# A hybrid decoder step on one core: cache pages one chunk sooner, two weight chunks back to back, Exps and merged values in other places

## What is computed

```python
xn = rms_norm(x, norm_w)
aq, ak, av, az, mq, mk, mv, mo, mz, ga, gm, mi, mf = split(xn @ w_in)
aq, ak = partial_rope(rms_norm(aq)), partial_rope(rms_norm(ak))
attn = moba(aq, ak, av)                     # samples: q . cached keys, top 3 of 4 blocks, softmax, cached values
h, (C, n, m) = mlstm_chunk(...)             # C_new = a * C + k v, h = q C / max(|q n|, exp(-m))
h = rms_norm(h * sigmoid(mo))
y_att = (attn * silu(az)) @ w_proj_attn
y_ml  = (h * silu(mz)) @ w_proj_mlstm
y = x + (sigmoid(ga) * y_att + sigmoid(gm) * y_ml) @ w_out
```

## Time and profile before

| | |
|---|---|
| median of three runs | 494.61 us |
| the profiled execution's own time | 493.16 us |
| its span in the trace | 491.4 us |
| TensorE matmul, busy | 464.9 us, 95% |
| VectorE busy | 403.6 us, 82% |
| ScalarE busy | 290.2 us, 59% |
| GpSimd busy | 102.2 us, 21% |
| the chain that ended last | TensorE 66%, VectorE 21%, ScalarE 5%, issue 4%, DMA 3% |

### The profile page before, as it was taken

The page is one execution under the profiler, slowest core; times in us unless marked ns, Lnnn a source line. Parts: engine busy times, 40 slices in busy tenths (PEclk is TensorE's granted clock), DMA queues, the critical chain, the costliest instruction groups (busy, mean ns, idle before and its releaser), DMA issues.

```text
span 491.4 us, 11313 instructions
## 1 busy us (share of the span) xinstructions
PE 464.9 (95%) x3848; PEld 422.5 (86%) x3848; DVE 403.6 (82%) x1650; ACT 290.2 (59%) x486; POOL 102.2 (21%) x182
## 2 busy tenths in 40 slices
PE   3899997999989999998999999999999999989997
PEld 2699897899869899887899889799989898889997
DVE  2988859799999889979889889889999864657861
ACT  2776544577884466795456595666678367324430
POOL 2032121102323213332421323222223210000000
PEclk9999999899999999999999999999999999999999
DMA  8498567847899998999988999997999995354511
GB/s 310 168 378 301 209 246 258 305 173 241 305 419 412 394 343 286 356 418 391 413 333 300 365 410 397 414 383 273 349 420 414 412 415 228 147 222 173 192 63 45
DMA packets 36409, 150.87 MB, mean 307 GB/s; under 512 B 5232, under 2 KB 6772, under 8 KB 29056
## 3 DMA queue, kind: packets, MB, share of 16 engines
q1 hardware_dynamic: 12160, 70.77, 37.6%
q0 software_dynamic: 19040, 67.20, 36.0%
q10 hardware_dynamic: 5152, 12.18, 6.4%
HBM read 137.37 MB, written 12.76 MB: 306 GB/s over the span
## 4 chain that ended last, share of the span: by engine, by line
PE 66%; DVE 21%; ACT 5%; issue 4%; DMA 3%; POOL 0%; ACTq 0%; POOLq 0%; DVEq 0%
PE pj L506 24%; PE pj L509 12%; PE wk L506 8%; DVE kpages L1127 7%; DVE w L1020 5%; PE pa L699 4%; PE wk L509 4%; PE wk L611 2%; PE wk L482 2%; DMA qbc<-q_dram 2%; PE wk L643 1%; DVE cslot L1213 1%; ACT L796 1%; ACT w L775 1%; DMA mlg<-in_tokens 1%
## 5 line engine op out<-in xcount | busy, mean ns | idle before, releaser
L506 PE MATMUL pj<-xn,w 128*128 128x264 f32 x1344 | 187.3, 292 | 3.6 <-issue 2.0
L506 PEld LDWEIGHTS pj<-xn,w 128*128 128x128 f32 x1344 | 171.9, 190 | 16.0 <-issue 11.7
L1020 DVE TENSOR_TENSOR w<-wraw,w 128x1024 fp32r<-128x1024 f32 x112 | 138.0, 1233 | 13.2 <-ACT w L775 12.7
L775 ACT ACTIVATE w<-wraw 128x1024 fp32r<-128x1024 f32 x112 | 117.7, 1052 | 24.0 <-PE wk L509 12.8
L1127 DVE CUSTOM_DVE_ANT_0 kpages<-kpages,qbc 128x128 f32<-128x128 f32 x512 | 115.6, 290 | 6.6 <-POOL qbc L415 4.7
L509 PE MATMUL pj<-xn,w 128*128 128x264 f32 x672 | 94.8, 284 | 0.0
L509 PEld LDWEIGHTS pj<-xn,w 128*128 128x128 f32 x672 | 86.5, 188 | 0.0
L399 POOL DMA_DIRECT2D kpages<-in_cache_k x64 | 34.3, 536 | 190.5 <-DVE sco L1127 157.9
L399 POOL DMA_DIRECT2D vpages<-in_cache_v x64 | 34.0, 531 | 60.7 <-issue 40.5
L1127 DVE DVE_READ_ACCUMULATOR2_ANT sco<- 128x1 f32 x512 | 41.7, 81 | 0.0
L699 PE MATMUL pa<-vpages,prob 128*32 128x256 f32 x512 | 34.3, 385 | 0.4 <-ACT prob L834 0.3
(11 more groups left out here) (262 smaller groups left out, 626.7 us busy)
## 6 DMA issues: line engine op xcount, KB each, us to landing
wraw<-in_weights SPq DMA_DIRECT2D x56, 1024.0 KB, 7.9
kpages<-in_cache_k POOLq DMA_DIRECT2D x64, 512.0 KB, 8.5
vpages<-in_cache_v POOLq DMA_DIRECT2D x64, 512.0 KB, 10.3
cslot<-in_states SPq DMA_DIRECT2D x16, 512.0 KB, 11.0
out_C_s<-cslot ACTq DMA_DIRECT2D x16, 512.0 KB, 9.9
xres<-in_tokens SPq DMA_DIRECT2D x1, 1056.0 KB, 7.6
out_k_p<-kT ACTq DMA_DIRECT2D x4, 256.0 KB, 11.0
out_v_p<-v_nat ACTq DMA_DIRECT2D x4, 256.0 KB, 4.4
```

The source lines that it names most:

```text
L506: mm(bank[:, 0:T], w2[:, q, 0, k, :], src[:, g, k, :], start=(k == 0 and g == 0), stop=False)
L775: A(w2[:, n % WSPLIT, 0], wraw[:, pair % WRAW, :, (n % 2) * P:(n % 2 + 1) * P], ACT.Copy).then_inc(whi_ready, 1)
L1020: V.tensor_tensor(w2[:, q, 1], wraw[:, slot, :, half * P:(half + 1) * P], w2[:, q, 0], ALU.subtract).then_inc(wlo_ready, 1)
```

## The change

Seven edits:

- START goes from 3 to 2 and all lags up by one: the key pages move one chunk sooner, everything behind them stays at its g.
- GpSimd spreads the first query straight from `qs` in SBUF, before it waits for the DRAM copy; the second query is spread inside the loop, at g = 4.
- In the body TensorE keeps the old order for g = 0 and 1. From g = 2 on it does P(g) and P(g + 1) for even g, then S(g) and S(g + 1) (`beside`).
- P(96), the first chunk of the output projection, goes slice by slice: for each k two products of the high weight and one of the low.
- ScalarE's three Exps at i = 1 come after the copy out of the chunk and the next `split_hi`.
- `merged_values` comes ahead of the gate product of g = 87.
- The wait counts of `q_row` follow from the second edit.

```diff
@@ -81,8 +81,8 @@
 
 
 
-START, PERIOD = 3, 9
-SUMS, SELECT, SHIFT, EXP, VALUES, TOTAL, GATHER, COLUMNS, OUT = 8, 9, 10, 11, 12, 14, 19, 20, 21
+START, PERIOD = 2, 9
+SUMS, SELECT, SHIFT, EXP, VALUES, TOTAL, GATHER, COLUMNS, OUT = 9, 10, 11, 12, 13, 15, 20, 21, 22
 
 
 def due(g, lag):
@@ -411,7 +411,7 @@
                 pool.dma_start(qbc[0:1, b % 2, :], q_dram[b:b + 1, :]).then_inc(q_row[b % 2], 16)
 
             def spread_queries(b):
-                pool.wait_ge(q_row[b % 2], 16 * (b // 2 + 1))
+                pool.wait_ge(q_row[b % 2], 16 * ((b + 1) // 2))
                 nc.gpsimd.partition_broadcast(qbc[:, b % 2, :], qbc[0:1, b % 2, :]).then_inc(q_spread, 1)
 
             def decay_rows(j):
@@ -442,13 +442,13 @@
             spread_rows(0)
             pool.wait_ge(qs_ready, 2)
             pool.dma_start(q_dram, qs[:, :]).then_inc(q_put, 16)
+
+            nc.gpsimd.partition_broadcast(qbc[:, 0, :], qs[0:1, :]).then_inc(q_spread, 1)
             pool.wait_ge(q_put, 16)
-
+            queries(1)
+
+            pool.wait_ge(q_spread, 1)
             values(VSLOTS - 1)
-            queries(0)
-            queries(1)
-            spread_queries(0)
-            spread_queries(1)
 
             for g in range(LAST):
                 b = due(g, SELECT)
@@ -461,7 +461,7 @@
                         keys(s + KSLOTS)
                     if s % PAGES == 0 and 2 <= s // PAGES + 1 < NB:
                         queries(s // PAGES + 1)
-                    if s % PAGES == 2 and 2 <= s // PAGES + 1 < NB:
+                    if s % PAGES == 2 and s // PAGES + 1 < NB:
                         spread_queries(s // PAGES + 1)
                 pair = value_pair(g)
                 if pair is not None:
@@ -498,6 +498,15 @@
 
                 pe.wait_ge(whi_ready, n + 1)
                 q = n % WSPLIT
+                if src is mrg2 and parts:
+                    pe.wait_ge(wlo_ready, n + 1)
+                    for k in range(KC):
+                        pe.wait_ge(parts, k + 1)
+                        mm(bank[:, 0:T], w2[:, q, 0, k, :], src[:, 0, k, :], start=(k == 0), stop=False)
+                        mm(bank[:, 0:T], w2[:, q, 1, k, :], src[:, 0, k, :], start=False, stop=False)
+                        last = mm(bank[:, 0:T], w2[:, q, 0, k, :], src[:, 1, k, :], start=False, stop=(k == KC - 1))
+                    last.then_inc(proj, 1)
+                    return
                 for k in range(KC):
                     if parts:
 
@@ -700,9 +709,8 @@
                                       vpages[:, s % VSLOTS, q * VW:(q + 1) * VW], start=(pg == 0), stop=(pg == PAGES - 1))
                         last.then_inc(v_used, 1)
 
-            for g in range(BODY):
-                pe.wait_ge(evac, HEADS + g - 1)
-                project(pj[g % 2], HEADS + g, xn2)
+            def beside(g):
+
                 if g == 0:
                     pe.wait_ge(q_ready, HEADS)
                     query_rows(pa[1], 0)
@@ -720,6 +728,15 @@
                 keys_side(g // CHUNKS, g % CHUNKS)
                 states_side(g // CHUNKS, g % CHUNKS)
                 cache_side(g)
+
+            for g in range(BODY):
+                pe.wait_ge(evac, HEADS + g - 1)
+                project(pj[g % 2], HEADS + g, xn2)
+                if g < 2:
+                    beside(g)
+                elif g % 2:
+                    beside(g - 1)
+                    beside(g)
 
 
             banks = [pj[0], pj[1], wk[1], wk[2]]
@@ -852,12 +869,6 @@
                 if g == 1:
                     act.wait_ge(wN_in, 1)
                     A(wN[:, :, :], gN[:, 3:6, :], ACT.Exp).then_inc(wN_ready, 1)
-                if i == 1:
-                    act.wait_ge(wl_ready, j + 1)
-                    u = [uT[:, t, j:j + 1] for t in range(2)]
-                    A(emt, emt, ACT.Exp)
-                    A(wt[:, 0:SEQ], wt[:, 0:SEQ], ACT.Exp, bias=u[0])
-                    A(wt[:, SEQ:384], wt[:, SEQ:384], ACT.Exp, bias=u[1]).then_inc(w_ready, 1)
                 if i in (2, 4):
                     n2 = i // 2 - 1
                     act.wait_ge(mlg_ready, j)
@@ -934,6 +945,12 @@
                     act.wait_ge(proj, n + 1)
                     A(dst, pj[n % 2][:, 0:T], ACT.Copy, scale=MHD ** -0.5 if i // 2 == 2 else 1.0).then_inc(evac, 1)
                 split_hi(n + AHEAD)
+                if i == 1:
+                    act.wait_ge(wl_ready, j + 1)
+                    u = [uT[:, t, j:j + 1] for t in range(2)]
+                    A(emt, emt, ACT.Exp)
+                    A(wt[:, 0:SEQ], wt[:, 0:SEQ], ACT.Exp, bias=u[0])
+                    A(wt[:, SEQ:384], wt[:, SEQ:384], ACT.Exp, bias=u[1]).then_inc(w_ready, 1)
                 if i == 0 and j:
                     output_gate(j - 1)
 
@@ -1357,6 +1374,8 @@
                 cache_side(BODY + i)
                 if key_page(BODY + i) is not None:
                     score_page(key_page(BODY + i))
+                if i == 23:
+                    merged_values()
                 if i == 12:
                     token_scores()
                 if i in (4, 6):
@@ -1379,8 +1398,6 @@
                     V.tensor_tensor(sgm[:, c, :], sga[:, c, :], sgm[:, c, :], ALU.add).then_inc(ywk, 1)
                 if i == 21:
                     merged_samples()
-                if i == 23:
-                    merged_values()
                 if i > 4 * KC:
 
                     c = i - 4 * KC - 1
```

## The result

| | before | after |
|---|---|---|
| median of the runs | 494.71 us (4 runs) | 481.79 us (4 runs, 481.07 to 482.34) |
| profiled execution, own time | 493.16 us | 482.34 us |
| span in the trace | 491.4 us | 480.2 us |

The kernel after takes 0.9735 of the time before (95% interval 0.9719 to 0.9752), 12.9 us less. The forecast was 483.1 us, 11.5 us less. The two profiled executions are 10.8 us apart: the one before lay 1.55 us under its median, the one after 0.55 us above.

The account below looks back on a forecast made before the run. TensorE was taken as the bound, with VectorE filling 92% of a job. Terms 4.6 + 4.0 + 2.1 + 0.8 = 11.5 us took 493.16 to 481.7 us; the median lies 1.45 us higher, so 483.1 us, range 476.4 to 490.1 us.

Parts of the forecast that it names:

- the rivals: Four outcomes: DMA holds 485.8 us, VectorE keeps up 476.4, head start eaten 491.7, slower 499.9; chances 0.16, 0.12, 0.10, 0.06.
- Term A: Job 0, first query spread directly: the 3.13 us wait in S(8) and the slow clock behind it go, 4.6 us.
- two slacks: Before S(8) in job 0: VectorE 2.7 us ahead, S(8) itself 3.1 us later, together 5.8 us against the wait.
- Term B: Jobs 1 to 3: early pages, pairs and moved Exps give 4.0 us, three eighths of the top; bounds 0 to 10.7.
- the top: Most that jobs 1 to 3 could gain: 4.6 + 1.3 + 1.5 + 2.7 + 0.6 = 10.7 us.
- the returns: TensorE going from small products back to a projection: pairs remove 27 of 31, at 0.10 us each, 2.7 us.
- the Exps: ScalarE's three Exps behind the copy that P(19) and P(35) wait for: up to 1.5 us go.
- The rival in which VectorE keeps up: VectorE's idle 19.0 us shrink with the rest, all 10.7 us of jobs 1 to 3 come: 476.4 us, chance 0.12.
- Terms C and D: Tail: merged values sooner, so P(88) starts 2.1 us sooner; slice-wise P(96) ends 0.8 us sooner.
- DMA rival: DMA holds jobs 2 and 3, so of jobs 1 to 3 only the first gains, 1.3 us: 485.8 us, chance 0.16.
- the forecast by it, 484.1 us: Skill's matmul gap rule: returns worth nothing, top 8.0 us, jobs 1 to 3 gain 3.0 us, time 484.1 us.

Follow-up runs that it names:

- e1: Kernel after with the pairs undone: TensorE does each chunk's small products directly behind that chunk again; 484.59 us.
- e2: Kernel before with the pairs alone added; 487.65 us.
- e4: Kernel after with the first query sent by way of DRAM again, the key pages still one chunk sooner; 484.31 us.
- e5: Kernel after with ScalarE's three Exps in front of the copy at i = 1 again; 481.29 us.
- e3: Kernel after with all key pages at their old chunks (START 3, old lags); 482.49 us.
- e11: Kernel after with ScalarE's copy of the chunk ahead of the norm at i = 2 and 4; 483.25 us.
- e8: Kernel after with page scores from 64 of 128 channels per head, so less VectorE work and a result that is not the reference's; 478.69 us.
- e10: Kernel after with key pages of samples 0 to 5 at their old chunks and those of 6 and 7 one chunk sooner; 478.47 us.
- e9: Kernel after storing only a 64th of the sample states, 7.3 MB of 151 MB less DMA traffic; 480.93 us.
- e13: Kernel after, unchanged, measured once more on a third chip; 481.2 us, in two groups, near 481 and above 484 us.
- e12: e10 with pairs in the tail too, for g = 64 to 85; 479.08 us.

## Why the prediction was right, and what in it was not

- **The sum.** 11.5 us forecast, 12.9 measured by the medians and 10.8 by the two profiled executions, against which the terms were made. The range held it, and none of the rivals came.
- **Term A, 4.6 us.** P(12) starts 5.1 us sooner; wait and slow clock went as told (L620 at 1.93 us). Between rows the wait is worth 3.3 us and the slow clock 1.7, because it goes on behind L611: from the first transposes of S(8) to P(9) it is 4.88 us before and 3.19 in e1. But of the two slacks I added up, 2.7 and 3.1 us, each was nearly enough alone: e1 has the first and e2 the second, and both gain the whole. The query edit was needed only because the pages came sooner (e4).
- **Term B, 4.0 us.** The three jobs take 226.4 instead of 230.2 us, 3.8 less. The number is right, the bookkeeping behind it is not, and that it came out is in part luck. Two terms of the top were worth next to nothing: the returns, 2.7 us, and the Exps, "up to 1.5 us" (e5). Three eighths of what is left of the top, 6.5 us, would have been 2.4 us. What came, taken two chunks at a time from P(12) to P(64), is a gain of 8.3 us, at P(20), P(38) and P(56) above all, less a loss of 4.2 us, at P(14) to P(18), P(24), P(32) and P(34). That the early pages and the pairs both free L675 was told, and either does it alone (e1, e3), so the second slack bought nothing there. The early pages cost 2.7 us up to P(64) and save 3.8 us at S(65), a place I did not look at. That the copy at i = 2 is late next was told, and the wait of 2.9 us there came, behind VectorE and not only behind the Exps (e11).
- **VectorE's side.** That VectorE takes back a part of B was right: most of the 4.2 us lost are waits for its low splits and what follows from them, and e8 gives it less to do and 3.7 us come by P(64), while TensorE's own work is unchanged. The rival in which VectorE keeps up would have needed that; my price for it, 6.7 us more than the forecast, was above what e8 found.
- **Why the early pages cost.** That they do is shown by e3 and e10, which put them back and gain 1.7 us by P(18) and 2.7 by P(64). The way is argued from the order: the step without a page moves from i = 11 to i = 10, so one page more lies at i = 11, ahead of VectorE's fullest steps, and P(15) and P(17) wait 0.47 and 1.12 us for low splits in the kernel after. TensorE in time, kernel after:

```profile
114.91 1.24 PE L518 MATMUL pj<-xn,w 128*128 128x264 f32 x8 [0.47 <-DVE w L1037]
...
124.47 1.25 PE L518 MATMUL pj<-xn,w 128*128 128x264 f32 x8 [1.12 <-DVE w L1037]
```

  In e3 and e10 these two waits are absent.
- **Terms C and D, 2.1 and 0.8 us.** P(88) starts 430.43 - 427.28 = 3.15 us after P(87) instead of 5.17: 2.0 us. P(96) takes 457.03 - 453.93 = 3.10 us instead of 3.97: 0.9 us.
- **DMA rival.** It gave jobs 2 and 3 nothing, and they take 1.2 and 0.9 us less. The share rose to 0.99, as it would, and the median did not care for 5% less traffic (e9). But the loads stand close behind: without the pairs TensorE waits 3.5 us for sample states (e1). And the one longer execution with a trace hangs on one small read (e13), which I had not considered.
- **Returns.** The readings of the rows were right: 16 matmuls behind a projection take 2.12 us and behind small products 2.2 to 2.3, before and after. Taking the difference for a cost was the mistake, since the longer row starts sooner: from start to start a dozen returns gave 0.2 us (e1), and three in the tail less than 0.1 (e12). e1 came out in the range that was worked out from 27 returns for another reason, the waits at S(24), S(40) and S(56). The rule of the Trainium skill (TensorE: Matmul & The Clock Gate, Back-to-back issue gap) has no term for what ran before, and on this point the traces agree with it; the forecast by it, 484.1 us, was still further off than mine, because my term for the returns made up for gains that I had put too low.

## What to carry to other kernels

When several edits each give the same wait more slack, the gains don't add: price the wait once, and ask of each edit what it does when the others are there. An edit that shifts work by a constant should be read at every place where its period meets another structure, above all where the loop ends: here one constant cost 2.7 us in the body and saved 3.8 us at its border, and taking it only where it pays (e10) gave 3 us more. If a second engine is over 90% busy, taking away one wait for it can just uncover the next (e5, e11); what helped here was less work on it (e8) and moving work out of its fullest stretch (e10). And price a change of order by the time from start to start over stretches that do the same work, not by how long a row lasts: rows overlap.

## What the runs showed of the hardware

A spread of 4 KB per partition on GpSimd took 1.29 us in the kernel before (the first of the two in the earlier trace rows), where VectorE was idle until its end. In the kernel after the first spread (L446, from `qs`) runs beside VectorE's work and takes 2.69 us, and VectorE's small product beside it (L1129, 8 x 96 elements) takes 1.20 us, 0.24 before. The Trainium skill (GPSIMD Engine Reference, Key points) says that the two share their SBUF interfaces and contend when VectorE has two SBUF inputs; the trace agrees, with a doubling of one and about a microsecond on the other. It is not the rule for every spread beside VectorE: the seven others in the kernel after (L415) take 1.29 to 1.72 us. I had priced the spread at 1.23 us, half of the row of two; the rest cost nothing here, since VectorE waited for ScalarE right behind it and started its first page without a wait.

The same read of 1 KB (L424) landed 2.5, 4.7, 7.5 and 10.6 us after its issue in one execution (e13), at a DMA share around it of 0.08, 0.40, 0.94 and 1.00. The last one, 1.9 us later than in the first trace of the same kernel, was followed by 3.5 us lost on TensorE between P(51) and P(53).
